# Early expert ids, feature-major row sums and modulation rows moved forward in a two-block transformer kernel

## Chip, cores and metric

The kernel runs on one core of a Trainium2 chip. The metric is the device time of one execution in microseconds, the median of several runs.

## The reference

A first block (attention with a causal mask, short convolution, PEER experts) is followed by a second block (feed-forward, retention with a context, Fourier branch, feed-forward). Everything is float32; 256 tokens and 256 context tokens of width 1024. All steps that are scaled, shifted or gated take their vectors from `silu(c) @ w_ada`: 12 pieces of 512 columns in the first block, 18 in the second. What the change touches:

```python
mod = jax.nn.silu(c) @ w_ada + b_ada
shift1, scale1, gate1, shift2, scale2, gate2 = jnp.split(mod, 6, axis=-1)
h = rms_norm(x, norm1_w) * (1.0 + scale1) + shift1
proj = h @ w_in                      # q, k, v, cb, cc, cx, iq, ik, iw
...
x = x + gate1 * (y_mix @ w_out)
h2 = rms_norm(x, norm2_w) * (1.0 + scale2) + shift2

# peer_ffn(h2), for each block of 128 tokens
q = (hb @ peer_wq).reshape(B, Q_BLOCK, PEER_HEADS, 2, PEER_HALF)
s = jnp.einsum('bqhpd,hpnd->bqhpn', q, peer_subkeys)
vals, idx = lax.top_k(s, PEER_TOPK)                  # 16 of 128 keys, twice
top_s, pos = lax.top_k(combo, PEER_TOPK)             # 16 of 256 pairs
expert = jnp.take_along_axis(ids, pos, axis=-1)      # 8 heads x 16 experts a token
g = jax.nn.softmax(top_s, axis=-1)
a = jax.nn.gelu(jnp.einsum('bqhkd,bqd->bqhk', peer_u[expert], hb))
y = jnp.einsum('bqhk,bqhkd->bqd', g * a, peer_v[expert])

x = x + gate2 * y
# second block begins: ctx and x each go through
x = x + 0.5 * g1x * swiglu(modulate(rmsnorm(x, norm_ffn1), sh1x, sc1x), w13_ffn1, w2_ffn1)
```

## The kernel before, in words

Activations lie feature-major, `x_t[feature within block, k, token]` with eight blocks `k` of 128 features. **Weights** stream through a ring of 2 MB slabs that SyncE (SP) loads in a fixed order, `slab_order`: SP waits until the slab that used the slot has been read and then issues one load. Slabs of `w_in`, `w_out` and `peer_wq` are split in four pieces each into a high part (ScalarE, `split_until`) and a low part (POOL before the gather, VectorE behind it), and each product is three matmuls. The order in which TensorE reads slabs is written out in its program; ScalarE's program repeats the same order for its copies out of PSUM.

**Modulation rows.** Each of the 30 pieces of `silu(c) @ w_ada` is a slab and a *row*: `mod_row_of(m)`, 8 matmuls of 32x512 (16 records, `psum<-ring,silu`). Rows are gathered in groups of two to four (`ROW_GROUPS`); when a group is complete and the next row has been done, `mod_turn` turns the group with 4 small matmuls (`psum<-early,small`) so that the vectors lie on partitions. `mod_steps(m0, m1)` does rows and the due turns. Rows 0 to 3 stand ahead of the input projection (`iq`, `q`, `k`, `v`, `cc`, `cx`, `cb`), rows 4 to 9 in it, 10 and 11 around the norm behind the output projection (`wo`), 12 to 17 between the four steps of the expert query (`pq`); row 18 (`SPARE`) has a slab of its own in `gap_slab[1]`, and 19 to 21 are ring slabs behind the query.

**Choice of the experts.** VectorE's `choose_experts(t)` handles one token tile of 128 in four groups of two heads (`top16`, the comparisons at L1769 and L1770), then computes all 128 ids a token (L1772) and publishes them (L1773, semaphore `ids`).

**Gather.** POOL copies eight ids a time (L1007) and issues one indirect DMA for each expert slot (L1017): 128 tokens, 8 KB each, 1 MB, 256 in all. Each row of `experts` holds `u` (first half) and `v` (second half). There are eight row buffers; a buffer comes free through `row_free_pe` (even rows) and `row_free_dve` (odd rows). The first tokens on both are given by VectorE ahead of the first dot, behind waits for the last key product and for row 18. Two rows make a batch, 128 batches. For a batch VectorE does two dots (L1838, `u` times `h2`), ScalarE the gelu (L1356), the gates (L1331) and a diagonal matrix of the even row's weights (L1335), TensorE adds the even row's `v` into two PSUM banks (2 matmuls of 128x512, token-major) and VectorE adds the odd row's into `y_of[t]` (L1845). At a tile's end VectorE adds the PSUM banks to `y_of[t]` (L1869), TensorE transposes the sum (`expert_turn`, L766) and VectorE adds it to `x_t` (`expert_residual`, L1792).

Between batches each engine takes steps of the **context's** feed-forward and of its `k` and `v` projections (108 chunks, `context()` on each engine), and VectorE the choice for the second tile. `ctx` itself is loaded by SP when the last `peer_wq` slab has been read.

**Tail.** Behind the gather come `squares_by_block("x1")` (8 matmuls with a matrix of ones, from ScalarE's squares, L1143), a root (L1035) and a reciprocal (L1488), row 22 out of `gap_slab[0]`, and the first feed-forward of the second block. Its first slab is loaded when the last even expert row has landed; then the gap slabs (each waits for both tokens of the buffers it overlays); then four loads of constants and two more slabs. Every matmul is issued through `mm` (L437).

```python
for half, bank in enumerate(sum_banks[t]):
    last = mm(psum[:, bank, :], diag[:, n % (GBUF // 2), :],
              rows[BATCH * n % GBUF][:, D + half * BANK:D + (half + 1) * BANK], b == 0, b == PER_TILE - 1)
last.then_inc(sem("row_free_pe"), 1)
```

## Time and profile before

| | us |
|---|---|
| median of 3 runs | 1847.63 (1844.91 to 1849.25) |
| the profiled execution, its own time | 1845.29 |
| its span, first to last instruction | 1843.5 |
| TensorE busy | 1619.5 (88%) |
| VectorE busy | 1219.8 (66%) |
| ScalarE busy | 701.6 (38%) |
| POOL busy | 452.2 (25%) |
| DMA, mean rate | 292 GB/s, 538.22 MB |

Engines in rows are PE (TensorE), PEld (its weight loads), DVE (VectorE), ACT (ScalarE), POOL (GpSimd), SP (SyncE). All times count from the span's start. Busy time in a row of matmuls counts records, which may be two for one instruction (`x16` are 8 matmuls). In brackets stands how long the engine was idle before an instruction, and what ended that. The gather runs from about 292 to 1050 us.

### The profile page before, as it was taken

What the parts mean: (1) busy time and instruction counts of PE and PEld (TensorE: products, weight loads), DVE (VectorE), ACT (ScalarE), POOL (GpSimd) and SP (SyncE); (2) the same over time, 40 slices, a digit from 0 to 9 for tenths busy, and PEclk for the clock granted to TensorE, in tenths of its full rate; (3) what the DMA queues carried; (4) which work ended last, traced back from release to release, by engine and by line L of the source; (5) the groups of instructions that cost most, each with busy time, mean ns of one, the idle gap of its engine ahead of it and who ended that gap; (6) DMA issues with size and microseconds to landing.
All of it is one profiled execution on the core that took longest, in us unless ns stands there. A gap on an engine that the chain in (4) does not pass through costs nothing.

```text
span 1843.5 us, 25165 instructions
## 1 busy us (share of the span) xinstructions
PE 1619.5 (88%) x9708; PEld 1296.9 (70%) x9708; DVE 1219.8 (66%) x1967; ACT 701.6 (38%) x1266; POOL 452.2 (25%) x342
## 2 busy tenths in 40 slices
PE   5999993888879878776998699999999999999997
PEld 3987771555646555544533289998999895989997
DVE  3795486887888877567577756565458447566554
ACT  4544342332233221123222356745443441444443
POOL 1664443443434534434445200000000000000000
PEclk8999996899989988888999799999999999999999
DMA  8556888999999999999999956645545550346542
GB/s 365 183 216 275 354 346 354 376 421 421 405 420 412 418 421 418 422 422 384 422 420 420 404 226 258 246 160 179 217 142 187 197 189 19 137 143 229 190 160 102
DMA packets 58001, 538.22 MB, mean 292 GB/s; under 512 B 6432, under 2 KB 6560, under 8 KB 7712
## 3 DMA queue, kind: packets, MB, share of 16 engines
q1 hardware_dynamic: 21024, 268.22, 37.4%
q0 software_dynamic: 36864, 268.45, 35.3%
q8 instruction: 76, 1.25, 0.3%
q14 instruction: 37, 0.30, 0.0%
HBM read 535.60 MB, written 1.05 MB: 291 GB/s over the span
## 4 chain that ended last, share of the span: by engine, by line
PE 51%; DMA 23%; DVE 14%; issue 7%; ACT 3%; POOL 1%; SPq 0%; POOLq 0%; DVEq 0%; ACTq 0%
PE psum L437 51%; DMA arena<-in_experts,idx_stage 20%; DVE arena L1845 2%; DMA ring<-in_w_ada 1%; POOL arena L1017 1%; DMA ring<-in_peer_wq 1%; DVE arena L1653 1%; DVE ring_r L1432 1%; DVE small L1770 1%; DMA ring<-in_w_in 0%; DVE arena L1769 0%; DMA ring<-in_w_ffn 0%; ACT h_t L1294 0%; ACT ring_r L1050 0%; DVE h_t L1512 0%
## 5 line engine op out<-in xcount | busy, mean ns | idle before, releaser
L1432 DVE TENSOR_TENSOR ring_r<-ring,ring_r 128x1024 fp32r<-128x1024 f32 (+1 forms) x240 | 287.0, 1207 | 270.9 <-ACT ring_r L1050 269.6
L437 PE MATMUL psum<-arena,small 128*128 128x512 f32 x544 | 303.5, 690 | 161.2 <-ACT small L1335 158.2
L1838 DVE CUSTOM_DVE_ANT_0 arena<-arena 128x1024 f32<-128x1024 f32 x256 | 313.8, 1226 | 179.7 <-DMA arena<-in_experts,idx_stage 174.3
L437 PE MATMUL psum<-small_r,ring_r 128*128 128x256 f32 x2304 | 415.6, 284 | 7.2 <-DVE h_t_r L1518 7.0
L1017 POOL DMA_INDIRECT arena<-in_experts,idx_stage x256 | 306.2, 1196 | 371.2 <-DVE arena L1845 172.1
L437 PEld LDWEIGHTS psum<-small_r,ring_r 128*128 128x128 f32 x2304 | 355.2, 189 | 14.8 <-issue 14.5
L1050 ACT ACTIVATE ring_r<-ring 128x1024 fp32r<-128x1024 f32 (+1 forms) x240 | 246.4, 1041 | 229.0 <-PE psum L437 178.4
L437 PE MATMUL psum<-arena_r,ring_r 128*128 128x256 f32 x2208 | 328.5, 283 | 3.2 <-DVE arena_r L1497 2.8
L437 PE MATMUL psum<-h_t_r,ring_r 128*128 128x256 f32 x1152 | 322.8, 280 | 0.0
L437 PEld LDWEIGHTS psum<-arena,small 128*128 128x128 f32 x544 | 111.5, 215 | 295.2 <-ACT small L1335 169.9
L437 PEld LDWEIGHTS psum<-arena_r,ring_r 128*128 128x128 f32 x2208 | 291.8, 190 | 3.8 <-DVE arena_r L1497 3.2
L1356 ACT ACTIVATE small<-small 128x2 f32<-128x2 f32 x128 | 26.0, 203 | 513.1 <-DVE small L1838 513.1
L437 PEld LDWEIGHTS psum<-h_t_r,ring_r 128*128 128x128 f32 x1152 | 218.7, 190 | 0.1
L437 PEld LDWEIGHTS psum<-h_t,ring 128*128 128x128 f32 x848 | 164.5, 194 | 52.2 <-issue 27.7
L437 PE MATMUL psum<-h_t,ring 128*128 128x256 f32 x848 | 195.4, 384 | 2.7 <-ACT h_t L1294 2.7
L1845 DVE SCALAR_TENSOR_TENSOR arena<-arena,small 128x1024 f32<-128x1024 f32 x128 | 164.5, 1285 | 4.6
L995 POOL TENSOR_TENSOR ring_r<-ring,upper 128x1024 fp32r<-128x1024 f32 x50 | 127.4, 2572 | 134.3 <-ACT upper L1050 94.7
L437 PE MATMUL psum<-arena_r,upper 128*128 128x256 f32 x768 | 144.0, 290 | 12.9 <-DVE arena_r L1518 8.4
L437 PEld LDWEIGHTS psum<-arena_r,upper 128*128 128x128 f32 x768 | 123.1, 196 | 16.6 <-issue 8.8
L437 PEld LDWEIGHTS psum<-arena,ring 128*128 128x128 f32 x352 | 70.2, 199 | 22.8 <-issue 13.9
L437 PE MATMUL psum<-arena,ring 128*128 128x256 f32 x352 | 83.6, 391 | 0.0
L1073 ACT ACTIVATE arena<-psum 128x512 f32<-128x512 f32 (+2 forms) x91 | 48.1, 545 | 76.6 <-PE psum L437 61.0
(234 smaller groups left out, 1416.4 us busy)
## 6 DMA issues: line engine op xcount, KB each, us to landing
ring<-in_w_ffn SPq DMA_DIRECT2D x33, 2048.0 KB
ring<-in_w_in SPq DMA_DIRECT2D x31, 2048.0 KB
ring<-in_w_ada SPq DMA_DIRECT2D x27, 2048.0 KB
ring<-in_w_ffn SPq DMA_DIRECT2D x24, 1408.0 KB
ring<-in_w_out SPq DMA_DIRECT2D x4, 2048.0 KB
ring<-in_peer_wq SPq DMA_DIRECT2D x4, 2048.0 KB
ring<-in_p_ret SPq DMA_DIRECT2D x4, 2048.0 KB
arena<-in_w_ada SPq DMA_DIRECT2D x3, 2048.0 KB, 12.7
```

Source lines behind the costliest of these rows:

```text
L437: return nc.tensor.matmul(o, a, b, start=first, stop=last)
L995: nc.gpsimd.tensor_tensor(whole(i, ring_r), whole(i, ring), upper(i).bitcast(F32), ALU.subtract).then_inc(lo_made, 1)
L1017: nc.gpsimd.indirect_dma_start(rows[slot % GBUF], None, dram["experts"], bass.IndirectOffsetOnAxis(ap=idx_stage[:, slot:slot + 1], axis=0) ...
L1050: nc.scalar.activation(upper(i), whole(i, ring), ACT.Copy).then_inc(hi_made, 1)
L1073: drain(nc.scalar.activation(dst, take(name)[:, 0:width], func, scale=scale))
L1356: nc.scalar.activation(acts[:, n % 8, :], dots[:, n % 8, :], ACT.Gelu_apprx_tanh).then_inc(sem("gelus"), 1)
L1432: nc.vector.tensor_tensor(whole(i, ring_r), whole(i, ring), upper(i).bitcast(F32), ALU.subtract).then_inc(lo_made, 1)
L1653: step(nc.vector.reciprocal(rs, rs))
L1770: step(nc.vector.tensor_reduce(hid_[:, a, some], hot, AX_X, ALU.add))
L1838: step(nc.vector.tensor_tensor_reduce(u, u, h2[:, n // PER_TILE, :], 1.0, 0.0, ALU.mult, ALU.add, dots[:, n % 8, s:s + 1]), sem("dots"))
L1845: STT(y_of[t], rows[(BATCH * n + 1) % GBUF][:, D:2 * D], weights[:, n % 8, 1:2], y_of[t], ALU.mult, ALU.add).then_inc(sem("row_free_dve"), 1)
```

## The change

It has six parts.

1. **Rows move forward.** `SPARE` becomes 21. Rows 4 and 5 stand behind `v`, 6 and 7 behind `cx`, 8 behind `cb`, 9 ahead of and 10 and 11 behind the attention's products, 12 ahead of `wo`, 13 and 14 around the norm, 15 to 20 between the steps of the query. Only 21, with the slab of its own, stays behind it.
2. **Early ids.** For the first tile the ids of the first six heads are published when the third of four groups is chosen, the last two heads' when the fourth is. POOL walks over a list of id ranges. The first tokens for row buffers are given by ScalarE behind its copy of row 21.
3. **ctx over POOL.** The load of `ctx` becomes an indirect DMA of POOL with the index `lane`, ahead of its gathers.
4. **Feature-major sums.** The even row's `v` is the stationary operand in 8 blocks of 128x128, the diagonal matrix the moving one, so that the sum stands feature-major in PSUM. The odd rows' sum `y_of[t]` is added into the same banks by 8 products with the identity. VectorE's two additions go. The last batch is done row by row: its odd row is also added by TensorE, behind `expert_turn(1, False)`.
5. **Half of the squares early.** Squares, sum, root and reciprocal of `x1` for tokens 0 to 127 are done between the context's steps in the gather; the tail keeps those of tokens 128 to 255.
6. `gap_slab[1]` is loaded behind the last sum, `yt1_1`.

```diff
-SPARE, GAP = 18, 22
+SPARE, GAP = 21, 22
...
-    first = (mods[:4] + w_in(0) + [("w_idx", 0, KD * 136)] + w_in(1) + w_in(2) + w_in(3) + mods[4:5] + w_in(4) + w_in(5)
-             + mods[5:6] + w_in(6) + mods[6:10] + out_proj + mods[10:12] + peer(0) + mods[12:14] + peer(1)
-             + mods[14:16] + peer(2) + mods[16:18] + peer(3) + mods[SPARE + 1:GAP])
+    first = (mods[:4] + w_in(0) + [("w_idx", 0, KD * 136)] + w_in(1) + w_in(2) + w_in(3) + mods[4:6] + w_in(4) + w_in(5)
+             + mods[6:8] + w_in(6) + mods[8:13] + out_proj + mods[13:15] + peer(0) + mods[15:17] + peer(1)
+             + mods[17:19] + peer(2) + mods[19:21] + peer(3))
...
+        published = [[PH // 2 - 1, PH // 2], [PH // 2]]
...
-            def squares_by_block(tag, sq=sq2, summed=1):
+            def squares_by_block(tag, sq=sq2, summed=1, tokens=slice(0, L)):
...
-                    last = mm(o[:, 0:L], ones[:], sq[:, k, :], k == 0, k == KD - 1)
+                    last = mm(o[:, tokens], ones[:], sq[:, k, tokens], k == 0, k == KD - 1)
...
+            def add_row(t, g, turn, first, last):
+
+                for j in range(KD):
+                    ins = mm(summed(t, j), rows[g % GBUF][:, D + j * P:D + (j + 1) * P], diag[:, turn % (GBUF // 2), :],
+                             first and j % 4 == 0, last and j % 4 == 3)
...
+            def expert_turn(t, last):
 
                 pe.wait_ge(sem("experts"), t + 1)
-                for i in range(2):
-                    o = begin(f"yt{t}_{i}", "dve")
-                    for j in range(4):
-                        last = nc.tensor.transpose(o[:, j * P:(j + 1) * P],
-                                                   y_of[t][:, (4 * i + j) * P:(4 * i + j + 1) * P], ident)
-                    ctx_end(f"yt{t}_{i}", last)
+                for j in range(KD):
+                    ins = mm(summed(t, j), y_of[t][:, j * P:(j + 1) * P], ident, False, last and j % 4 == 3)
...
+                pe.wait_ge(sem("sq_x1_first"), 1)
+                o = begin("ss_x1_first", "act")
+                for k in range(KD):
+                    last = mm(o[:, 0:P], ones[:], sq_first[:, k, :], k == 0, k == KD - 1)
...
-                for half, bank in enumerate(sum_banks[t]):
-                    last = mm(psum[:, bank, :], diag[:, n % (GBUF // 2), :],
-                              rows[BATCH * n % GBUF][:, D + half * BANK:D + (half + 1) * BANK], b == 0, b == PER_TILE - 1)
-                last.then_inc(sem("row_free_pe"), 1)
...
+                add_row(t, BATCH * n, n, b == 0, False).then_inc(sem("row_free_pe"), 1)
...
-            expert_turn(1)
-            squares_by_block("x1")
+            expert_turn(1, False)
+            pe.wait_ge(sem("diag"), BATCHES + 1)
+            add_row(1, BATCH * BATCHES - 1, BATCHES, False, True)
+            squares_by_block("x1", tokens=slice(P, L))
...
+            pool.wait_ge(sem("lane"), 1)
+            pool.wait_ge(*slab_free[slabs.index(("peer_wq", 3, SLAB))])
+            nc.gpsimd.indirect_dma_start(ctx_t.rearrange("p k t -> p (k t)"), None, dram["ctx"],
+                                         bass.IndirectOffsetOnAxis(ap=lane, axis=0)).then_inc(sem("ctx_landed"), 16)
...
+            lists = [(t, b0 * 2 * PSEL // ROUND, b1 * 2 * PSEL // ROUND) for t in range(NT)
+                     for b0, b1 in zip([0] + published[t], published[t])]
+            for known, (t, r0, r1) in enumerate(lists):
+                pool.wait_ge(sem("ids"), known + 1)
...
             mod_row_of(SPARE)
+            act.sem_inc(sem("row_free_pe"), GBUF // 2)
+            act.sem_inc(sem("row_free_dve"), GBUF // 2 + 1)
...
+                yield done_at["yt0_1"] + 2
+                act.wait_ge(*emptied("yt0_1"))
+                nc.scalar.activation(sq_first, x_t[:, :, 0:P], ACT.Square).then_inc(sem("sq_x1_first"), 1)
...
-                step(nc.vector.reciprocal(rstd[:], rstd[:]))
+                fresh = rstd[:, P:L] if tag == "x1" else rstd[:]
+                step(nc.vector.reciprocal(fresh, fresh))
...
+                    if g + 1 in published[t]:
+                        known = slice(([0] + published[t])[published[t].index(g + 1)] * 2 * PSEL, (g + 1) * 2 * PSEL)
+                        step(STT(id_f[:, known], hid_[:, 0, known], float(PK), hid_[:, 1, known], ALU.mult, ALU.add))
+                        step(nc.vector.tensor_copy(ids[:, t * SLOTS + known.start:t * SLOTS + known.stop], id_f[:, known]),
+                             sem("ids"))
                     yield
-                step(STT(id_f, hid_[:, 0, :], float(PK), hid_[:, 1, :], ALU.mult, ALU.add))
-                step(nc.vector.tensor_copy(ids[:, t * SLOTS:(t + 1) * SLOTS], id_f), sem("ids"))
...
-                    for half, bank in enumerate(sum_banks[t]):
-                        y = y_of[t][:, half * BANK:(half + 1) * BANK]
-                        step(TT(y, y, psum[:, bank, :], ALU.add), sem("experts") if half else chain)
```

How it moves instructions, first on TensorE between the last input slab (`cb`) and the first product of the output projection. Before (`ring,silu` is a modulation row, `early,small` a turn, `early,h_t` the turned probabilities, `arena,ones` a sum of squares, `arena` 128x128 the attention's products):

```order
L437 MATMUL psum<-ring,silu 32x512 x8
L701 MATMUL psum<-early,h_t 128x128 x16
L437 MATMUL psum<-ring,silu 32x512 x8
L437 MATMUL psum<-arena 128x128 x12
L437 MATMUL psum<-arena,ones 128x256 x4
L437 MATMUL psum<-arena 128x128 x12
L437 MATMUL psum<-ring,silu 32x512 x8
L437 MATMUL psum<-early,small 128x4 x4
L437 MATMUL psum<-arena,ones 128x256 x4
L437 MATMUL psum<-ring,silu 32x512 x8
L437 MATMUL psum<-arena_r,upper_53 128x256 x2
```

With the change, for the same stretch:

```order
L442 MATMUL psum<-ring,silu 32x512 x8
L442 MATMUL psum<-early,small 128x4 x4
L707 MATMUL psum<-early,h_t 128x128 x16
L442 MATMUL psum<-ring,silu 32x512 x8
L442 MATMUL psum<-arena 128x128 x12
L442 MATMUL psum<-arena,ones 128x256 x4
L442 MATMUL psum<-arena 128x128 x12
L442 MATMUL psum<-ring,silu 32x512 x8
L442 MATMUL psum<-early,small 128x2 x4
L442 MATMUL psum<-ring,silu 32x512 x8
L442 MATMUL psum<-arena,ones 128x256 x4
L442 MATMUL psum<-ring,silu 32x512 x8
L442 MATMUL psum<-early,small 128x2 x4
L442 MATMUL psum<-arena_r,upper_53 128x256 x2
```

Between the attention's products and the sum of squares stand two rows (10 and 11) where one stood (8). One turn has become three: that of rows 4 to 7 has gone ahead of the probabilities, and those of 8 and 9 and of 10 and 11 are new here, the last of them directly ahead of the output projection.

SP's queue around the last `w_in` slab, before (each row a load, in brackets what it waits for):

```order
L964 DMA ring<-in_w_in 128x4096 [waits group_done] x2
L964 DMA ring<-in_w_ada 128x4096 [waits group_done]
L964 DMA ring<-in_w_in 128x4096 [waits group_done] x2
L964 DMA ring<-in_w_ada 128x4096 [waits group_done]
L964 DMA ring<-in_w_in 128x4096 [waits piece_done]
L964 DMA ring<-in_w_ada 128x4096 [waits group_done] x2
L964 DMA ring<-in_w_ada 128x4096 [waits piece_done]
L964 DMA ring<-in_w_ada 128x4096 [waits group_done]
L964 DMA ring<-in_w_out 128x4096 [waits piece_done]
L964 DMA ring<-in_w_out 128x4096 [waits group_done]
```

With the change:

```order
L980 DMA ring<-in_w_in 128x4096 [waits group_done] x2
L980 DMA ring<-in_w_ada 128x4096 [waits group_done] x2
L980 DMA ring<-in_w_in 128x4096 [waits group_done] x2
L980 DMA ring<-in_w_ada 128x4096 [waits piece_done] x2
L980 DMA ring<-in_w_in 128x4096 [waits group_done]
L980 DMA ring<-in_w_ada 128x4096 [waits group_done]
L980 DMA ring<-in_w_ada 128x4096 [waits piece_done]
L980 DMA ring<-in_w_ada 128x4096 [waits group_done] x2
L980 DMA ring<-in_w_ada 128x4096 [waits piece_done]
L980 DMA ring<-in_w_out 128x4096 [waits group_done]
L980 DMA ring<-in_w_out 128x4096 [waits piece_done]
```

Two modulation slabs instead of one stand ahead of the last `w_in` slab, and five (rows 8 to 12) instead of four (rows 6 to 9) between it and `w_out`.

The end of the gather on TensorE, before: the last context products (`ring,h_t`), the rest of the row sums, the transposes (L766), the sum of squares of `x1` and row 22.

```order
L437 MATMUL psum<-ring,h_t 128x512 x4
L437 MATMUL psum<-arena,small 128x512 x20
L766 MATMUL psum<-early,arena 128x128 x8
L437 MATMUL psum<-small,ones 128x256 x8
L437 MATMUL psum<-arena,silu 32x512 x8
```

With the change (80 are ten even rows of eight products, `early,arena` adds the odd rows' sum, the next eight add the last odd row):

```order
L442 MATMUL psum<-ring,h_t 128x512 x4
L442 MATMUL psum<-small,arena 128x128 x80
L442 MATMUL psum<-early,arena 128x128 x8
L442 MATMUL psum<-small,arena 128x128 x8
L442 MATMUL psum<-small,ones 128x128 x8
L442 MATMUL psum<-arena,silu 32x512 x8
```

Each row of experts is eight products of 128x128 where it was two of 128x512, the transposes have become additions in the same banks, and the sum of squares has half of the columns.

## Rows read from the trace of the kernel before

**Rows 1.** Stretches: length, busy us (instructions) by engine, PEclk, DMA share, GB/s.
```profile
57.00:107.00 50.00, 48.93 (x347) 42.44 (x346) 46.92 (x77) 28.34 (x47) 35.27 (x14) 1.00 0.51 188
...
290.00:300.00 10.00, 0.00 (x0) 0.00 (x0) 1.44 (x5) 1.59 (x2) 3.91 (x5) 0.50 0.46 170
...
330.00:340.00 10.00, 8.73 (x19) 4.55 (x20) 9.79 (x24) 6.21 (x17) 3.88 (x4) 0.72 0.59 220
340.00:850.00 510.00, 417.89 (x1410) 277.82 (x1409) 391.53 (x673) 132.18 (x374) 217.93 (x193) 0.91 1.01 418
```

**Rows 2.** Timeline of PE: start us, us, operation, [idle before <-releaser].
```profile
107.23 0.37 PE L437 MATMUL psum<-arena 64*128 64x128 f32 x1 [1.30 <-DVE arena L1654]
...
155.12 1.92 PE L437 MATMUL psum<-ring,silu 128*32 128x512 f32 x16
156.98 1.05 PE L437 MATMUL psum<-early,small 128*128 128x4 f32 x8
157.89 1.97 PE L437 MATMUL psum<-arena,ones 128*128 128x256 f32 x8
...
164.02 0.47 PE L437 MATMUL psum<-arena_r,upper 128*128 128x256 f32 x2 [2.31 <-POOL ring_r L995]
```

**Rows 3.** Timeline of DVE, end of the choice and first dots.
```profile
275.58 0.49 DVE L1721 MAX8 small<-arena 128x8 f32<-128x128 f32 x2
...
291.29 0.29 DVE L1777 TENSOR_TENSOR small<-small 128x128 f32<-128x128 f32 x1
301.00 1.23 DVE L1838 CUSTOM_DVE_ANT_0 arena<-arena 128x1024 f32<-128x1024 f32 x1 [9.42 <-DMA arena<-in_experts,idx_stage]
...
304.80 1.23 DVE L1838 CUSTOM_DVE_ANT_0 arena<-arena 128x1024 f32<-128x1024 f32 x1 [2.56 <-DMA arena<-in_experts,idx_stage]
...
319.78 1.23 DVE L1838 CUSTOM_DVE_ANT_0 arena<-arena 128x1024 f32<-128x1024 f32 x1 [1.17 <-DMA arena<-in_experts,idx_stage]
```

**Rows 4.** Timeline of POOL, first gathers.
```profile
292.00 0.19 POOL L1007 COPY idx_stage<-ids 128x8 uint32 x1 [29.83 <-DVEq L1829]
295.36 1.12 POOL L1017 DMA_INDIRECT arena<-in_experts,idx_stage  x1 [3.17 <-issue]
...
334.87 1.90 POOL L1017 DMA_INDIRECT arena<-in_experts,idx_stage  x1 [10.79 <-PE psum L437]
```

**Rows 5.** L1769, 230 to 292, then 292 to 680: ns min/median/max, start.
```profile
L1769 DVE TENSOR_TENSOR arena<-arena,small x8: 691/693/2769, 231.0 to 289.0; 128x512 f32<-128x512 f32 x8
L1769 DVE TENSOR_TENSOR small<-small x8: 691/692/693, 385.4 to 612.5; 128x512 f32<-128x512 f32 x8
```

**Rows 6.** Timeline of PE, and its group of row sums, 342 to 1040.
```profile
217.83 2.05 PE L437 MATMUL psum<-arena 128*128 128x128 f32 x16
219.63 0.48 PE L437 MATMUL psum<-arena_r,upper 128*128 128x256 f32 x2
...
989.33 1.88 PE L437 MATMUL psum<-arena,small 128*128 128x512 f32 x4
991.04 3.60 PE L437 MATMUL psum<-ring,h_t 128*128 128x512 f32 x8
...
994.48 1.88 PE L437 MATMUL psum<-arena,small 128*128 128x512 f32 x4
...
L437 PE MATMUL psum<-arena,small 128*128 128x512 f32 x483 | 269.4, 687 | 119.2 <-ACT small L1335 116.2 <-issue 3.0
```

**Rows 7.** Chain of waits (first line), then timelines of ACT, PE and DVE, the tail.
```profile
1042.00 8.19 DMA ring<-in_w_ffn
...
1054.09 2.54 ACT L1143 ACTIVATE small<-x_t 128x256 f32<-128x256 f32 x8
...
1054.63 5.92 PE L437 MATMUL psum<-small,ones 128*128 128x256 f32 x16 [2.92 <-ACT small L1143]
...
1061.17 1.75 DVE L1488 RECIPROCAL rstd<-rstd 128x256 f32<-128x256 f32 x1 [4.12 <-ACT rstd L1035]
```

**Rows 8.** The page, costliest groups: weight loads.
```profile
L437 PEld LDWEIGHTS psum<-small_r,ring_r 128*128 128x128 f32 x2304 | 355.2, 189 | 14.8 <-issue 14.5
```

143 lines of the change are left out of this document (85 added, 58 removed).

## The prediction

> **What bounds the kernel now.** I read the table of stretches first, then the timelines of TensorE, VectorE and GpSimd (POOL) at its edges. The span falls into three parts. In the **head**, up to about 290 us, TensorE is the bound: 48.93 of 50 us busy, with DMA at a share of 0.51 [rows 1]. In the **gather**, rows of the experts stream in; from 340 to 850 us DMA stands at 1.01 of its engines and 418 GB/s, while TensorE (417.89 of 510) and VectorE (391.53) have room [rows 1]. Between the two lies a hole: from 290 to 300 us DMA is at 0.46 and VectorE works 1.44 us of 10 [rows 1]. The gather therefore ends when its 256 MB are through, and starts when VectorE has published the expert ids. In the **tail**, behind 1042 us, a chain of short steps leads to the first feed-forward: slab, pieces, squares, root, reciprocal.
>
> **Head: three more rows ahead of the ids.** Rows 4 to 12 instead of 4 to 9 now stand before the output projection. One row of TensorE takes 156.98 − 155.12 = 1.86 us from start to start [rows 2], so three cost 5.6. The order shows two more turns before that projection and one fewer behind it. A turn is 1.05 us long and 157.89 − 156.98 = 0.91 from start to start; I take 1.0 where one is added and 0.9 where one is saved. One added turn lies right before the squares of attention and counts, +1.0. The other lies behind them, ahead of the output projection, where TensorE waits 2.31 us for POOL's pieces [rows 2]: nothing. The one that goes from behind the projection gives −0.9. Row 5 now stands before the second projection `cc`, and TensorE waits 1.30 us there for VectorE's mask [rows 2]; the row's 1.86 us fill that wait: −1.3. Sum +5.6 + 1.0 − 1.3 − 0.9 = +4.4, taken as **+4.5**. Bounds: +3, if the 2.31 us wait takes in more of it (row 12 moves ahead of that wait too), and +8, if a slab is late or the last `w_in` slab, now asked for behind two more rows, is split late (5.6 + 2.0 + some of a row). The three slabs' 6.3 MB take 15.0 us at the 418 GB/s of [rows 1]; 49% of 50 us idle at that stage hides them. The same rows vanish from behind the query, where nobody but DMA was short.
>
> **Ids and the first dots.** VectorE's last step of tile 0's choice starts at 291.29 and takes 0.29; the first dot starts at 301.00, after 9.42 us of waiting for a row; then come waits of 2.56 and 1.17 us [rows 3]. Now ids of three of four groups are published when the third group ends, 275.58 [rows 3], plus 0.5 us for the two added operations (under the 0.29 us each of the 128x128 operation at 291.29) plus 4.5 of head: about 280.6. POOL copied at 292.00 and issued at 295.36 with 3.17 us in between [rows 4]; the same from 280.6 on puts the first issue at 284, and with the 5.6 us from issue to dot seen before (301.00 − 295.36) the row is there at 289.6. VectorE is then the bound: it ends its choice at 291.6 + 4.5 + 0.5 = 296.6 and starts its dots then, 4.4 us before 301.00. The waits inside the first batches, 2.56 + 1.17 = 3.7, go as well, since rows have landed in all eight buffers. So the gather's state at its VectorE-bound stretch comes **8.1 us** earlier. That stretch is real: from 330 to 340 VectorE is busy 9.79 of 10 with DMA at 0.59, and POOL stands 10.79 us before 334.87 for a buffer that TensorE holds [rows 1, 4]. Behind it DMA is the bound, so the lead carries to the last row. Bounds: nothing, if a later token holds POOL, to −15.0 below.
>
> What speaks against this: while the fourth group is chosen, POOL now issues gathers. `L1769`, two of which stand in each group, took 0.69 us in the median but 2.77 once, in the stretch in which POOL still subtracts; with gathers running, from 292 to 680 us, all eight took 0.691 to 0.693 [rows 5]. So I add nothing. The Trainium skill, "SBUF — State Buffer", section "Who interferes with whom", says that a VectorE operation with two SBUF inputs contends with a GpSimd operation that reads SBUF, over a port that one holds at a time. If issuing a gather were such a read, the fourth group's two `L1769` would each grow by 2.1 us, and with 4.2 us less gain the kernel would come to 1840.2. The trace of the gather speaks against it.
>
> **Row sums with the features on the partitions.** For an even row TensorE now issues 8 products of 128x128, 16 records, in place of 2 of 128x512. 16 records of 128x128 took 219.63 − 217.83 = 1.80 us [rows 6]; the present four take 991.04 − 989.33 = 1.71 [rows 6]. So +0.1 us a batch, 128 batches, 12 us of work. TensorE idles 119.2 us before exactly these products from 342 to 1040 us [rows 6], so it costs nothing; without that cover it would cost 12. The period with a context chunk is now 994.48 − 989.33 = 5.15 us and would be 5.24; DMA's pace is (1042 − 301) / 128 = 5.8 us a batch, on average.
>
> **Tail.** The landing of the feed-forward slab holds: it is asked for at 1042.00 and is there 8.19 us later [rows 7], when the last even row is in; that doesn't move against the last row. ACT splits it and squares from 1054.09 on, 2.54 us; TensorE's sum of squares takes 5.92 from 1054.63; VectorE's reciprocal 1.75 [rows 7]. Half of the tokens are now done in the gather. TensorE: −5.92 / 2 = −3.0, of which I take 2.6, since it starts only with the first squares. VectorE: −0.9. ACT's squares run ahead of TensorE's sum and give nothing themselves. Sum **−3.5**, bounds −2 and −5. The row-by-row last batch and the dropped additions end earlier than before and are covered by the slab's landing. The second gap slab, asked for later, and ctx over POOL's queue move only loads with slack: nothing.
>
> **Sum.** +4.5 − 8.1 − 3.5 is −7.1 against the old times; but the 4.4 us at the first dot already hold the head's +4.5 (without it they would be 8.9). So the head is not counted twice: −8.1 − 3.5 = −11.6. From the profiled execution's 1845.3 that gives 1833.7; the median of the runs, 1847.6, lies 2.3 higher, so I forecast **1836.0**.
>
> **Rivals.**
> (a) The head costs 8 instead of 4.5 and half of the two waits stays: 3.5 + 1.9 = 5.4 us above the forecast, 1841.4. For it: POOL's queue of subtractions and the ring slots are tied to the row order. Against: a DMA share of 0.51. Chance 0.15.
> (b) DMA is the bound from the first row on. Then the three slabs of 15.0 us that leave the stretch behind the query count in full instead of 8.1: 1829.1. Against: the share of 0.59 at 330 to 340 [rows 1]. Chance 0.10.
> (c) The lead is lost. A token that comes late, or a batch in the VectorE-bound stretch that waits for something else, puts the gather back where it was; the tail remains at best, and a head that is longer eats it: 1844 to 1849. Chance 0.10. That the change doesn't do what it says belongs here: the early list would bring nothing if POOL sat behind its load of ctx.
> (d) **Slower.** The short products don't hide their weight loads. One load of 128x128 takes 189 ns [rows 8]. If 16 of them stood bare, a row's sum would cost 3.0 us, and TensorE's period with a chunk 3.44 + 3.0 = 6.5 us against DMA's 5.8. With 108 chunks and 20 batches without, 108 × 6.5 + 20 × 5.0 = 802 us against 741: +61 less 12, near 1896. It decides from 5.8 − 3.44 = 2.4 us a row on. Against it: the transposes of [rows 6], 112 ns a record with loads of the same size. The Trainium skill, "TensorE: Matmul & The Clock Gate", section "Back-to-back issue gap", gives some 81 ns for a sustained pair of load and product at 128 columns, where a lone product needs 56. Scaling the present 1.71 us by that ratio is 2.5 us, an estimate by that page, and would put the kernel just over the point. The row of 1.80 us is a direct measurement, so I give this 0.06.
>
> **How the numbers follow.** Forecast 0.59, (a) 0.15, (b) 0.10, (c) 0.10, (d) 0.06. The forecast's own bounds, from the head (+3.5, −1.5), the tail (±1.5) and the median (±2), are about 1831 to 1841. The range 1827 to 1846 adds (a), (b) and the better part of (c). 0.2% is 3.7 us, about what a measurement of this kernel can tell from no change: faster is below 1843.9, which holds the forecast, (a), (b) and a little of (c), less what of them could miss by more: 0.79. Same 0.12, from (c) and the upper end of (a). Slower 0.09, from (d) and a head that isn't paid back.
>
> **What would show it.** The first `L1838` at about 296.6, its second and fourth without a wait; POOL's first gather near 284; the last step of the choice 5 us later than before; a record of the 128x128 sums at 112 ns and TensorE's period below 5.3 us; still idle time of some 100 us before them; DMA at 1.0 from about 332; the last even row near 1034; TensorE's sum of squares for `x1` 3 us or less, the reciprocal 0.9. The prediction is wrong if TensorE is busy without gaps between 340 and 1030, if the choice ends later than 298, or if POOL's first gathers wait for a token.

## The result and the profile after

The change measured 1836.5 us (median of 5 runs, 1831.41 to 1842.43), against 1847.63 before. The ratio is 0.9935 with a 95% interval from 0.9919 to 0.9952. A repeat of the changed kernel gave 1835.29 against 1849.76, ratio 0.9923 (0.9910 to 0.9936). The forecast was 1836.0.

The profiled execution of the change took 1837.43 us (span 1835.6), only 7.9 less than that of before. Why the two profiles differ by less than the medians is taken up below: the profiled head of before was short, that of the change long.

The table of stretches of the changed kernel, with the columns of [rows 1]:

```profile
57.00:107.00 50.00, 50.00 (x359) 42.52 (x360) 45.72 (x77) 26.14 (x44) 32.76 (x13) 1.00 0.49 188
290.00:300.00 10.00, 0.00 (x0) 0.00 (x0) 9.59 (x33) 0.23 (x2) 5.73 (x6) 0.50 0.99 409
330.00:340.00 10.00, 7.98 (x55) 7.32 (x54) 9.76 (x27) 5.99 (x16) 4.36 (x5) 1.00 0.73 265
340.00:850.00 510.00, 420.25 (x2431) 380.31 (x2429) 389.52 (x671) 136.84 (x378) 215.49 (x191) 0.92 1.01 417
```

The hole at 290 to 300 us has gone: DMA at 0.99 instead of 0.46, VectorE at 9.59 us of 10 instead of 1.44. From 340 on the gather is DMA's as before. The head is the other side, still TensorE's. Its timelines around the output projection, first ScalarE, then TensorE (compare [rows 2]), then SP's issue of the `w_out` slabs:

```profile
165.45 2.00 ACT L1075 ACTIVATE upper<-ring 128x1024 fp32r<-128x1024 f32 x2 [4.09 <-DMA ring<-in_w_out]
...
164.09 1.99 PE L442 MATMUL psum<-arena,ones 128*128 128x256 f32 x8
166.01 1.92 PE L442 MATMUL psum<-ring,silu 128*32 128x512 f32 x16
168.20 1.05 PE L442 MATMUL psum<-early,small 128*128 128x2 f32 x8 [0.26 <-ACT small L1098]
172.49 0.47 PE L442 MATMUL psum<-arena_r,upper 128*128 128x256 f32 x2 [3.23 <-DVE arena_r L1548]
...
152.25 9.46 SPq L980 DMA_DIRECT2D ring<-in_w_out  x2
```

From the start of the attention's sum of squares to the first product of the output projection passed 6.13 us before (157.89 to 164.02) and pass 8.40 now (164.09 to 172.49). ScalarE stood 4.09 us for the slab of `w_out`. TensorE's wait ahead of the projection has grown from 2.31 to 3.23 us, although a turn was put into it.

VectorE, end of the third group's ids and the first dots (compare [rows 3]), and POOL (compare [rows 4]):

```profile
285.37 0.26 DVE L1825 SCALAR_TENSOR_TENSOR small<-small 128x96 f32<-128x96 f32 x1
285.67 0.21 DVE L1826 CAST ids<-small 128x96 uint32<-128x96 f32 x1
301.88 1.23 DVE L1891 CUSTOM_DVE_ANT_0 arena<-arena 128x1024 f32<-128x1024 f32 x1
303.15 1.23 DVE L1891 CUSTOM_DVE_ANT_0 arena<-arena 128x1024 f32<-128x1024 f32 x1
...
316.36 1.22 DVE L1891 CUSTOM_DVE_ANT_0 arena<-arena 128x1024 f32<-128x1024 f32 x1
323.87 1.22 DVE L1891 CUSTOM_DVE_ANT_0 arena<-arena 128x1024 f32<-128x1024 f32 x1
...
286.30 0.18 POOL L1032 COPY idx_stage<-ids 128x8 uint32 x1 [6.88 <-DVE ids L1826]
287.57 0.97 POOL L1042 DMA_INDIRECT arena<-in_experts,idx_stage  x1 [1.08 <-issue]
331.15 0.94 POOL L1042 DMA_INDIRECT arena<-in_experts,idx_stage  x1 [10.18 <-PE psum L442]
```

POOL copies ids 0.4 us after they are known and issues 1.3 us later, 14.3 us ahead of the first dot. No dot waits for a row up to 323.87; before, five of the first eight waited, 13.8 us in all (9.42, 2.56 and 1.17 of [rows 3], 0.43 and 0.26). POOL still stands 10.18 us for TensorE before 331.15. The choice ends directly ahead of the first dot, at 301.9: later than the 298 us behind which the prediction had called itself wrong. The section on why the forecast held takes this up.

The row sums on TensorE, one period with a context chunk and the group from 332 to 1031 us (compare [rows 6]):

```profile
900.21 1.95 PE L442 MATMUL psum<-small,arena 128*128 128x128 f32 x16
902.00 3.62 PE L442 MATMUL psum<-h_t,ring 128*128 128x256 f32 x16
...
907.24 3.60 PE L442 MATMUL psum<-ring,h_t 128*128 128x512 f32 x8
...
L442 PE MATMUL psum<-small,arena 128*128 128x128 f32 x1922 | 269.2, 300 | 112.1 <-ACT small L1366 111.9
```

Sixteen records take 1.79 us, the period is 907.24 − 902.00 = 5.24 us, and TensorE idles 112.1 us before these products.

The tail: SP, ScalarE, TensorE, VectorE (compare [rows 7]):

```profile
1039.13 0.33 SPq L980 DMA_DIRECT2D ring<-in_w_ffn  x1
1051.19 1.69 ACT L1168 ACTIVATE small<-x_t 128x128 f32<-128x128 f32 x8
1051.63 2.02 PE L442 MATMUL psum<-small,ones 128*128 128x128 f32 x16 [3.36 <-ACT small L1168]
1057.47 0.36 PE L442 MATMUL psum<-small_r,ring_r 128*128 128x256 f32 x1 [1.97 <-DVE h_t_r L1569]
1054.66 0.95 DVE L1539 RECIPROCAL rstd<-rstd 128x128 f32<-128x128 f32 x1 [1.53 <-ACT rstd L1060]
```

From the issue of the first feed-forward slab to its first product 22.77 us passed before (1042.00 to 1064.77), 18.34 now.

### The profile page after: what moved, and what is told of

It is laid out like the page before. It is cut to its first block, busy times and chain, and to the rows that moved or that the text cites. A ratio compares the mean times of both kernels' runs of the same rounds, so it can differ in the third digit from the quotient of the medians.

```text
span 1835.6 us, 28337 instructions
## 1 busy us (share of the span) xinstructions
PE 1621.9 (88%) x11292; PEld 1456.0 (79%) x11292; DVE 1212.0 (66%) x1968; ACT 704.7 (38%) x1272; POOL 447.5 (24%) x343
## 4 chain that ended last, share of the span: by engine, by line
PE 55%; DMA 22%; DVE 11%; issue 6%; ACT 4%; POOL 1%; SPq 0%; POOLq 0%; DVEq 0%; ACTq 0%
PE psum L442 54%; DMA arena<-in_experts,idx_stage 18%; DMA ring<-in_w_ffn 2%; DVE arena L1898 2%; DMA ring<-in_w_ada 1%; POOL arena L1042 1%; DMA ring<-in_peer_wq 1%; DVE ring_r L1482 1%; DMA ring<-in_w_out 1%; DVE arena_r L1548 1%; ACT ring_r L1075 1%; DVE small L1822 0%; DVE arena L1821 0%; ACT h_t L1321 0%; DVE h_t L1563 0%
## 5 line engine op out<-in xcount | busy, mean ns | idle before, releaser
L442 PE MATMUL psum<-small,arena 128*128 128x128 f32 x2064 | 292.4, 302 | 147.2 <-ACT small L1366 147.0
L442 PEld LDWEIGHTS psum<-small,arena 128*128 128x128 f32 x2064 | 280.3, 215 | 173.1 <-ACT small L1366 143.4
L1042 POOL DMA_INDIRECT arena<-in_experts,idx_stage x256 | 301.6, 1178 | 376.3 <-DVE arena L1898 166.7
L442 PEld LDWEIGHTS psum<-h_t,ring 128*128 128x128 f32 x848 | 160.3, 194 | 24.0 <-ACT h_t L1321 3.8
L1075 ACT ACTIVATE upper<-ring 128x1024 fp32r<-128x1024 f32 x52 | 53.6, 1053 | 62.8 <-DMA ring<-in_peer_wq 28.8
## 6 DMA issues: line engine op xcount, KB each, us to landing
ring<-in_w_ada SPq DMA_DIRECT2D x27, 2048.0 KB, 11.1
arena<-in_w_ada SPq DMA_DIRECT2D x3, 2048.0 KB, 12.6
```

Source lines behind the costliest of these rows:

```text
L442: return nc.tensor.matmul(o, a, b, start=first, stop=last)
L1042: nc.gpsimd.indirect_dma_start(rows[slot % GBUF], None, dram["experts"], bass.IndirectOffsetOnAxis(ap=idx_stage[:, slot:slot + 1], axis=0) ...
L1075: nc.scalar.activation(upper(i), whole(i, ring), ACT.Copy).then_inc(hi_made, 1)
```

## Experiments

Each was run on the chip beside the kernel before. For the comparisons below I use six places read from the timeline of every profile (us): modulation row 4, the last row ahead of the output projection, the first row behind it, VectorE's last cast of ids of tile 0, the first dot, and the dot of the last even row. Profiles of one kernel differ by up to 5 us in these places, so stretches between two places are compared, not the places themselves.

| profile | row 4 | last ahead | first behind | last ids | first dot | last even dot |
|---|---|---|---|---|---|---|
| before | 98.1 | 159.8 | 190.3 | 290.82 | 301.00 | 1042.16 |
| before, again | 99.6 | 161.3 | 191.8 | 295.95 | 306.30 | 1048.61 |
| rows only | 98.1 | 164.7 | 197.1 | 299.54 | 309.83 | 1051.82 |
| change | 99.4 | 166.0 | 200.6 | 301.13 | 301.88 | 1039.29 |
| change, again | 101.2 | 167.8 | 201.2 | 301.67 | 302.41 | 1039.99 |
| full squares | 99.6 | 166.2 | 197.9 | 297.12 | 297.87 | 1035.66 |
| ctx by SP | 98.0 | 164.6 | 197.1 | 297.71 | 298.46 | 1035.70 |
| late ids | 100.4 | 167.0 | 200.9 | 299.43 | 307.19 | 1050.57 |
| rows back | 99.5 | 161.2 | 194.3 | 294.91 | 295.65 | 1042.99 |
| choice later | 99.4 | 166.0 | 199.9 | 299.10 | 299.85 | 1036.67 |
| row 12 later | 99.8 | 162.7 | 195.4 | 303.65 | 304.39 | 1040.82 |
| pieces behind the root | 99.9 | 162.7 | 198.0 | 302.49 | 303.23 | 1040.92 |
| the same, choice later | 98.2 | 161.0 | 193.8 | 299.85 | 300.59 | 1035.97 |
| sums doubled | 99.7 | 166.3 | 201.3 | 301.42 | 302.16 | 1111.19 |

### The two kernels again

> The changed kernel itself once more, for a second profile and a better median. The profiled execution of the change is 7.9 us under that of before (1837.43 against 1845.29), the medians are 11.1 apart. Theory A (the profile is typical): the gain is 8 to 9 us. Theory B (the medians are typical): 11 to 12 us. In the profile, rows at the same places as in the first one within 0.5 us, except that the start of the head may differ by 1.3 us, since the fourth modulation row ran at a lower granted clock in one of the two profiles (3.29 us against 1.93).

Measured: 1835.29 (5 runs, 1834.17 to 1839.44), ratio 0.9923; its profiled execution took 1839.44. The medians are 14.5 us apart here, more than theory B had, and theory A is out. Single executions of the change ranged from 1831.4 to 1842.4, so one profiled execution says little about the gain. Row 4 stood 1.8 us later than in the first profile, where 1.3 had been allowed.

> The kernel before itself, for a second profile. Within one kernel the heads of the profiles so far differ by up to 4.5 us (first dot of the changed kernel at 301.9, 302.4 and 297.9), in two stretches: the first four rows (granted clock 0.81 to 0.92 up to 36 us) and the output projection (31.7 to 34.6 us from the last row before it to the first behind it). Theory A (the profile of before had a short head): this one has its row 4 at 99 to 101 us instead of 98.1 and that stretch longer than 30.5 us, and its first dot at 303 to 306 instead of 301.0. Theory B (the stretch is longer because of the moved rows): 30.5 us again within 0.5.

Measured: 1849.15 (12 runs), ratio 1.0005 (0.9994 to 1.0016), profiled 1848.3. Row 4 at 99.6 as theory A had it, and the first dot at 306.30, 5.3 us later than in the first profile. But the projection's stretch was 30.5 us again, as theory B had it; the other 3.6 us came behind it, between the first row behind the projection and the ids (104.1 us against 100.5). So the first profile's head was shorter than this one, and not in the place that I had named. What made the 3.6 us isn't shown. The first 36 us differ in the granted clock as well; rows back and then the change again, with a mean clock of 0.93 and 0.81 there, the columns as in [rows 1]:

```profile
0.00:36.00 36.00, 16.31 (x88) 7.68 (x88) 9.37 (x31) 11.02 (x16) 0.20 (x4) 0.93 0.96 399
0.00:36.00 36.00, 18.08 (x88) 8.14 (x88) 8.05 (x30) 10.31 (x15) 0.20 (x4) 0.81 0.95 400
```

Row 4 stands at 99.5 in the one and 101.2 in the other, with the same work ahead of it. The mean clock doesn't order the profiles, though: row 4 stood at 98.1 with 0.89 (before) and at 99.4 with 0.86 (change), so it is at most a part of the difference.

### The rows alone, and all but the rows

```diff
-SPARE, GAP = 18, 22
+SPARE, GAP = 21, 22
```
(the first experiment is the kernel before with this, the slab order and all `mod_steps` of the change; the second is the inverse edit on the changed kernel)

> The kernel before with only the modulation rows moved. Theory A (rows ahead of the query cost the head 4.9 us, and what they take off the DMA behind the query is worth nothing while the ids come late and nothing waits for DMA there): +3 to +6 us over before, 1852 to 1855. Theory B (the three slabs that leave the stretch behind the query are worth more than the head costs): 1840 to 1847.

Measured: 1856.38 (7 runs, 1852.63 to 1858.64), ratio 1.0040 (1.0026 to 1.0055), 7 us slower, 1 more than theory A had at most. From row 4 to the last row ahead of the projection it takes 66.6 us where before takes 61.7, +4.9, the same in every profile with all of the rows moved. The first dot still waits:

```profile
309.83 1.22 DVE L1838 CUSTOM_DVE_ANT_0 arena<-arena 128x1024 f32<-128x1024 f32 x1 [9.53 <-DMA arena<-in_experts,idx_stage]
```

and from the last ids to the last even dot pass 752.3 us, against 751.3 and 752.7 before. So the moved rows give nothing back while the ids are late. The slowdown is put down to the head, since nothing else in the table grew.

> Only the modulation rows go back to their old places (4 to 9 before the output projection, 18 with its own slab, 19 to 21 behind the query); all else stays as changed. Theory A (the head pays: the choice ended 9.6 us later with the rows moved, and that is what bounds the first dot): the choice ends at about 292 instead of 301.9, the gather ends some 5 to 8 us earlier than in the changed kernel, about 1829 to 1832 us. Theory B (the three slabs behind the query are worth their 15 us of DMA): first rows land late, the dots wait for them, and the time is that of the changed kernel or up to 7 us more.

Measured: 1837.94 (5 runs, 1837.04 to 1843.32), ratio 0.9938 (0.9925 to 0.9950), 1 to 3 us over the change by the medians, with intervals that overlap. The last ids came at 294.9, 3 us later than theory A had the end of the choice and 6 to 7 earlier than in the change; the gain did not come, as theory B had it. VectorE's second dot, and the stretches of DMA:

```profile
301.75 1.22 DVE L1891 CUSTOM_DVE_ANT_0 arena<-arena 128x1024 f32<-128x1024 f32 x1 [4.86 <-DMA arena<-in_experts,idx_stage]
...
290.00:300.00 10.00, 0.00 (x0) 0.00 (x0) 6.48 (x14) 1.94 (x4) 0.95 (x1) 0.50 1.01 432
300.00:330.00 30.00, 12.50 (x66) 11.46 (x67) 23.12 (x49) 9.58 (x23) 7.51 (x7) 0.67 1.01 418
330.00:340.00 10.00, 8.88 (x47) 8.33 (x47) 9.79 (x24) 5.54 (x14) 4.43 (x5) 0.78 0.48 170
```

The first dot starts 0.7 us behind the last ids, the second waits 4.86 us for its row, with DMA at 1.01: the gathers share it with the feed-forward slabs behind the three late rows (SP issues them from 271.3 to 284.3 us, in the change from 259.4 to 277.8). From the last ids to the last even dot pass 748.1 us, against 738.2 and 738.3 in the changed kernel and 751.3 before. Of the 13 to 14 us that early ids and moved rows win together there, early ids alone (with the other parts of the change) win 3 to 5, moved rows alone none. In the whole time the rows also cost the head some 5 us, so that moving them is worth 1 to 3 us net, which these runs don't tell from nothing.

### Early ids

```diff
-        published = [[PH // 2 - 1, PH // 2], [PH // 2]]
+        published = [[PH // 2], [PH // 2]]
```

> Only the early list of ids goes: the first tile's ids are published once, when the fourth group is chosen. Theory A (the early list brings the whole gain at the start): the first gather is issued at about 303, the first dot waits until 308 to 310 instead of starting at 301.9, the waits of 2.6 and 1.2 us inside the first batches come back, and the time rises by 9 to 12 us, to about 1847. Theory B (the gather is bound by its row buffers at 315 to 331 us anyway): less than 4 us more.

Measured: 1847.39 (12 runs, 1844.1 to 1853.8), ratio 0.9987 (0.9976 to 0.9998): 12 us over the change's repeat, 11 over its first median. VectorE's first dots:

```profile
307.19 1.23 DVE L1891 CUSTOM_DVE_ANT_0 arena<-arena 128x1024 f32<-128x1024 f32 x1 [7.00 <-DMA arena<-in_experts,idx_stage]
310.50 1.23 DVE L1891 CUSTOM_DVE_ANT_0 arena<-arena 128x1024 f32<-128x1024 f32 x1 [2.07 <-DMA arena<-in_experts,idx_stage]
```

Theory A, at its upper end. The first gather was issued at 301.4, the first dot starts at 307.2, and from the last ids to the last even dot pass 751.1 us. Rows only, which also lacks parts 3 to 6, took 752.3 there: these parts are worth about 1 us in that stretch, no more than profiles of one kernel differ there.

### Squares of all tokens in the tail

```diff
-            squares_by_block("x1", tokens=slice(P, L))
+            squares_by_block("x1")
-            norm_hi("x1", 2, mod2_v[:, 0, :, 0], ["yt1_0", "yt1_1"], tokens=slice(P, L))
+            norm_hi("x1", 2, mod2_v[:, 0, :, 0], ["yt1_0", "yt1_1"])
...
-                fresh = rstd[:, P:L] if tag == "x1" else rstd[:]
+                fresh = rstd[:]
```

> The tail squares, sums and roots all 256 tokens again; the early half is computed and not used. Theory A (half of the work is half of the time, as forecast): +3.5 us, TensorE's sum of squares near 5.9 us again. Theory B (TensorE's 5.92 us before were the lower clock; behind the new row-by-row products it is at full clock, and its sum only follows ScalarE's squares): TensorE's sum under 3 us with all columns, ScalarE +0.9, VectorE +0.8, in all +1.7 us.

Measured: 1838.83 (6 runs, 1831.12 to 1842.7), ratio 0.9938 (0.9917 to 0.9959); the interval reaches from 1 us under the change's repeat to 7 over it, so the place is read from the trace. TensorE's sum of squares, then the first product:

```profile
1047.97 5.25 PE L442 MATMUL psum<-small,ones 128*128 128x256 f32 x16 [4.40 <-ACT small L1168]
1057.44 0.36 PE L442 MATMUL psum<-small_r,ring_r 128*128 128x256 f32 x1 [2.37 <-DVE h_t_r L1569]
```

The slab was issued at 1035.51, so 21.93 us passed to that product, against 18.34 and 19.04 in the change: +3.2. Theory A, by the size. On the clock both theories were too simple. With all columns the sum took 5.25 us, with a mean granted clock of 0.70 over it; with half of them it took 2.02 at 1.00 in the first profile of the change, but in the second it lost the clock too (0.63):

```profile
1052.51 3.05 PE L442 MATMUL psum<-small,ones 128*128 128x128 f32 x16 [3.70 <-ACT small L1168]
```

### The price of the row sums

```diff
-                add_row(t, BATCH * n, n, b == 0, False).then_inc(sem("row_free_pe"), 1)
+                add_row(t, BATCH * n, n, b == 0, False)
+                add_row(t, BATCH * n, n, False, False).then_inc(sem("row_free_pe"), 1)
```

> The changed kernel with the eight products of every even row issued twice into the same banks (the even rows are then added twice). It prices the cover over the row sums. Theory A (16 records take 1.8 us at full clock and nothing shows of them beside DMA): the added 128 x 1.8 = 230 us are 118 more than TensorE's 112 us of idle time before these products, so the time rises by 110 to 140 us, TensorE without gaps, DMA's share in the gather down to 0.86. Theory B (weight loads stand bare once products follow each other): a pair of sums takes over 4.8 us, and the time rises by 200 us or more.

Measured: 1909.93 (2 runs), ratio 1.0332 (1.0306 to 1.0358). Timeline of TensorE, the group of row sums from 340 to 1090 us, and the stretch of [rows 1]:

```profile
900.87 3.73 PE L442 MATMUL psum<-small,arena 128*128 128x128 f32 x32
904.44 3.62 PE L442 MATMUL psum<-h_t,ring 128*128 128x256 f32 x16
...
L442 PE MATMUL psum<-small,arena 128*128 128x128 f32 x3742 | 438.6, 277 | 12.6 <-ACT small L1367 12.6
...
340.00:850.00 510.00, 510.00 (x3597) 482.92 (x3596) 363.64 (x636) 123.82 (x350) 185.22 (x176) 1.00 0.97 389
```

32 records take 3.57 us, 112 ns each, so theory B falls. The idle time is down to 12.6 us and TensorE is busy for all of 510 us. But the time rose by 74 us over the change, not by 110 to 140, and DMA's share fell to 0.97, not 0.86. TensorE's mean granted clock from 340 to 850 us went from 0.92 to 1.00. From 340 us to the last context products and sums TensorE was busy for 577.5 of 691 us in the change and for 744.7 of 761 here: 167 us more, for added products of 128 × 1.79 = 229. The other 62 us were saved by records that had run at the lower clock (a record of the sums took 140 ns on average in the change, 117 here), and gaps took up 97. The cover over the row sums is larger than the idle time in the trace.

### ctx over SP

```diff
-            nc.gpsimd.indirect_dma_start(ctx_t.rearrange("p k t -> p (k t)"), None, dram["ctx"],
-                                         bass.IndirectOffsetOnAxis(ap=lane, axis=0)).then_inc(sem("ctx_landed"), 16)
...
+                if replaced is not None and slabs[replaced][:2] == ("peer_wq", 3):
+                    sp.dma_start(ctx_t.rearrange("p k t -> p (k t)"), dram["ctx"]).then_inc(sem("ctx_landed"), 16)
```

> The changed kernel with ctx loaded by SP again, behind the third feed-forward slab. Forecast: nothing (within 1.5 us). The rival: POOL's first gather was held by its load of ctx, which waits for the last peer_wq slab (POOL idles 6.4 us before it at 278.3), so without it POOL is ready earlier; but the first gather waits for the ids at 285.7 in any case.

Measured: 1834.93 (4 runs), ratio 0.9923 (0.9901 to 0.9945), the same as the change's repeat. The forecast holds: ctx over POOL neither costs nor gains.

### Attempts at a faster one

```diff
-    return (n + 1) * 2 // 5
+    return max(0, (n - 7) // 2)
```

> The changed kernel, with VectorE's choice for the second token tile begun at batch 9 instead of batch 2 and done a little faster, so that 5 us of it leave the stretch from 315 to 340 us. Theory A (VectorE bounds the gather's first 45 us, DMA idles 6 us in them): the DMA-bound state comes 4 to 5 us earlier and the time falls by as much, to 1831. Theory B (TensorE's late release of the row buffers bounds there: POOL waited 10.2 us for it before 331.2): less than 1.5 us gained.

Measured: 1834.5 (6 runs, 1831.65 to 1834.7), ratio 0.9919 (0.9904 to 0.9934), within the interval of the change. The ninth dot came 19.5 us behind the first instead of 22.0, yet from the last ids to the last even dot pass 737.6 us instead of 738.3. By this profile theory B: of a lead of 2.5 us, 0.7 is left. The last run of this section has the same edit and kept more.

```diff
-             + mods[6:8] + w_in(6) + mods[8:13] + out_proj + mods[13:15] + peer(0) + mods[15:17] + peer(1)
+             + mods[6:8] + w_in(6) + mods[8:12] + out_proj + mods[12:15] + peer(0) + mods[15:17] + peer(1)
...
-            mod_steps(12, 13, False)
...
-            mod_steps(13, 14)
+            mod_steps(12, 14)
```

> The changed kernel with row 12 and the turn ahead of the output projection moved behind it. Theory A (the first w_out slab lands late, at 164 instead of 154.5 us, since five modulation slabs are loaded ahead of it at 5 us each while TensorE uses a row up in 1.9): it lands 5 us earlier, the output projection begins 2 to 4 us earlier against row 11, and after the row's own 1.9 us the ids come 0.5 to 2 us earlier. Theory B (a row costs its 1.86 us wherever it stands): no change of the ids, within 0.5 us.

Measured: 1840.47 (6 runs), ratio 0.9952 (0.9933 to 0.9971), by the medians 4 to 5 us slower than the change, with intervals that still overlap. TensorE at the projection and at the norm, ScalarE at the norm:

```profile
168.72 0.47 PE L442 MATMUL psum<-arena_r,upper 128*128 128x256 f32 x2 [2.21 <-DVE arena_r L1546]
205.89 1.65 PE L442 MATMUL psum<-arena,ones 128*128 128x256 f32 x3 [5.14 <-ACT arena L1167]
...
203.53 2.00 ACT L1074 ACTIVATE upper<-ring 128x1024 fp32r<-128x1024 f32 x2 [11.95 <-DMA ring<-in_peer_wq]
```

The projection begins 6.1 us behind row 11 instead of 10.3, and ScalarE no longer waits for `w_out`: theory A's first half, though 2.9 of the 4.2 us are only the row and the turn that have gone from there. But the first `peer_wq` slab now lands one slab later, ScalarE waits 11.95 us for it with two squares of the norm behind it in its queue, and TensorE waits 5.14 for these. From row 4 to the last ids pass 203.8 us, against 201.7 and 200.5 in the change: the ids come later, not earlier.

The next run's edit, against this one:

```diff
-                    between={KD - 2: lambda: split_until(first_peer + 1), KD: lambda: mod_steps(12, 14)})
+                    between={KD: lambda: mod_steps(12, 14), "root": lambda: split_until(first_peer + 1)})
```

> Row 12 behind the output projection as in the run before, and ScalarE's first two pieces of peer_wq are split behind the norm's root instead of ahead of its last two squares. Theory A (in the run before, ScalarE stood 11.95 us for that slab with two squares behind it, and TensorE 5.1 us for them; the slab's place in the queue is the cost): TensorE's wait of 5.1 us goes, the query's first product comes at 207 to 209 for a row 11 at 162.5, the ids come 1 to 3 us earlier than in the changed kernel, about 1833. Theory B (the pieces are then late for the query instead): the query waits for POOL, and nothing is gained.

Measured: 1840.92 (6 runs), ratio 0.9956 (0.9939 to 0.9973). The wait at the norm has gone, and this one has come ahead of the query:

```profile
213.03 0.77 PE L442 MATMUL psum<-arena_r,upper 128*128 128x256 f32 x2 [6.95 <-DVE arena_r L1569]
```

Nothing is gained, as theory B had it, but not for its reason: TensorE waits for VectorE, and ScalarE did not wait for the slab when it began its pieces (206.16). The time went into VectorE's first three steps of `h_t`, here beside POOL's subtractions of these pieces, and below in the change, without them:

```profile
207.04 5.45 DVE L1563 SCALAR_TENSOR_TENSOR h_t<-x_t,cols,rstd 128x256 f32<-128x256 f32 x3
207.30 4.91 POOL L1013 TENSOR_TENSOR ring_r<-ring,upper 128x1024 fp32r<-128x1024 f32 x2 [15.39 <-ACT upper L1074]
...
206.87 1.28 DVE L1563 SCALAR_TENSOR_TENSOR h_t<-x_t,cols,rstd 128x256 f32<-128x256 f32 x3
```

They took 5.45 us instead of 1.28, 4.2 us that stand directly ahead of the query. The wait for the slab itself had gone.

> The run before plus the later choice for the second tile, the version meant to beat both kernels. By the two effects (1 to 3 us, and 0.8 us from the last ids to the last even row as measured): 1831 to 1834.

Measured: 1839.55 (6 runs, 1834.08 to 1841.72), ratio 0.9952 (0.9935 to 0.9969): the forecast of 1831 to 1834 failed, since the first of its two effects had not come. The ninth dot again came 19.5 us behind the first, and from the last ids to the last even dot pass 736.1 us, against 738.4 in the run that it is built on: here 2.3 of the 2.5 us were kept. No version beat the change by more than its interval.

## Why the forecast held, point by point

**The total** is right, to 0.5 us against the first median, and the sum was of the right terms; that it is so close is in part luck. For a profiled execution of the change the prediction had 1833.7, and the profile took 1837.43. It had also called itself wrong if the choice ended later than 298 us. The choice ended at 301.9 and 302.4, and with it the first dot came 5 us later than forecast (301.9 for 296.6) and the last even row as well (1039.3 for 1034). So by its own sign the head is where it was wrong. A part of the 5 us is the profiles: the first profile of before had its last ids at 290.8, the second at 296.0, and both of the change lie some 2 us above the average of the heads with moved rows. With all profiles the terms are these.

**Head, forecast +4.5 (bounds 3 to 8).** Between row 4 and the last row ahead of the projection the moved rows cost 4.9 us, in each profile. My terms up to there were 5.6 + 1.0 + 0 − 1.3 = 5.3. The last ids of seven heads with these rows in the table (rows only, the change twice, full squares, ctx by SP, late ids, choice later) stand at 299.4 on average; before, twice, at 293.4. With 0.4 us of it for the added operations of early ids that is +5.6 for the head, 1 us over the forecast (with the head of the doubled sums as an eighth, +5.9). As single heads of one kernel lie up to 5 us apart, the 1 us is not clear of noise; the wait that it contains is. **The step that failed** is that 49% of idle DMA hides the slabs. From the start of the last row ahead of the projection to the projection's first product 4.2 us pass in both profiles of before, and 5.1 to 6.9 in the eight with moved rows. Five modulation slabs in a row, 5 us of DMA each (2.1 MB at 418 GB/s), stand ahead of `w_out`; TensorE uses a row up in 1.86 us. SP asked for `w_out` at 152.25 instead of 144.22, and the slab was there 13 us later; ScalarE waited 4.09 us for it, and the turn that I put down as free, inside the 2.31 us wait, was not. The idle DMA lay elsewhere: in the change its share was 0.69 and 0.47 from 110 to 120 and to 130 us, while SP waited for slots of the ring, and 0.92 to 1.01 from 150 to 165, when `w_out` was on its way. The first experiment with row 12 shows that it is the slab's place in the queue: with one slab fewer ahead of `w_out` the projection starts earlier, and the wait has moved to `peer_wq`, the next slab that is needed. The second removes that wait and meets another, of VectorE beside POOL.

**Start of the gather, forecast −8.1.** From the last ids to the last even dot: 751.3 and 752.7 before, 738.2 and 738.3 (full squares 738.5, ctx by SP 738.0) after, −13.8. Less the head and the added operations (+6.0) that is −7.8. The mechanism is as forecast: no dot waits for a row, the choice itself is the bound, and without the early list all of it goes (+12 us). What the forecast did not have is that it needs both parts: with the rows back in place the ids come 5 us sooner, but the gathers then share DMA with slabs that come behind three late rows. In the forecast I had left that DMA without a price in the sum; rival (b) had put 15 us on it. The experiment puts 9.8 us on it (748.1 against 738.3), less 5 for the head; by the medians 1 to 3 us of that remain.

**Row sums, forecast nothing.** 1.79 us a row and a period of 5.24 were forecast to 0.01, and the 112.1 us of idle time are there. Rival (d) fell on both: 112 ns a record also when they follow without a gap. No run takes the row sums alone back; that they cost nothing rests on the idle time, on their price with doubled sums and on late ids against rows only. The ratio of a sustained pair to a lone product that the Trainium skill gives at 128 columns ("TensorE: Matmul & The Clock Gate", "Back-to-back issue gap"), from which I had the 2.5 us, does not show here: the measured 1.79 decides.

**Tail, forecast −3.5 (2 to 5).** From the slab's issue to the first product 22.8 and 23.9 us before, 18.3 and 19.0 after, −4.7. Halved squares are 3.2 of it by experiment. Some 1.0 of the other 1.5 lies in the same sum of squares: with all columns it took 5.92 and 6.58 us before, at a granted clock of 0.62 in the first, against 5.25 at 0.70 in that experiment. From the slab's issue to ScalarE's first piece nothing moved (8.3 and 8.5 us before, 8.3 after). ctx over POOL costs nothing, as forecast.

**Sum.** −7.8 − 4.7 = −12.5, against −11.6 forecast and −11.1 and −14.5 measured by the two pairs of medians. The sum leaves out everything behind the first feed-forward product, 778.7 and 774.1 us before, 778.1 and 778.7 in the change. That stretch differs by 4.6 us between two profiles of one kernel, so the sum is no better than a few us, and its closeness to the medians proves no single term.

**What an early lead is worth.** The forecast said that a lead at the VectorE-bound stretch carries to the last row. For the change it did. All that the change won there it had by the ninth dot: 36.5 and 36.3 us behind the last ids before, 22.7 in both profiles of the change; from there to the last even dot pass 714.9 and 716.4 before, 715.4 and 715.6 now. The later choice made 2.5 us there and kept 0.7 in one run and 2.3 in the other. Profiles of the change without that edit lie between 737.2 (row 12 later) and 738.5 us from the last ids to the last even dot, so two profiles can't settle whether this lead carries. Why the first kept less I haven't shown.

## What to carry to other kernels

A weight slab in a ring costs its transfer time in the place where it stands, not on the average of the stretch: ahead of a slab that is needed soon, count slabs times their 5 us against the engine's use of them, and don't read idle DMA as cover. In one stretch two edits can be worth nothing and 3 to 5 us alone, and 13 together, when one removes the wait and the other clears the transfers that would take its place; test the pair and each alone, and set against it what each costs elsewhere (here 5 us of head). And when two single profiles are compared, compare each stretch from its own start, and take a second profile of the kernel before: its head alone differed by 5 us.

## What was not expected of the hardware

TensorE's granted clock rose with its load. In the gather it was 0.92 with 112 us of idle time, 1.00 with the sums doubled; the added 230 us of work cost 74. The sum of squares in the tail ran at 126 ns a record (2.02 us for 16) with half of the columns in the first profile of the change, 3.36 us of idle time ahead of it, and at 191 (3.05 us) in the second, with 3.70 ahead; with all columns and 4.40 ahead it ran at 328 (5.25 us). The granted clock over these sums was 1.00, 0.63 and 0.70.

VectorE's operation with two inputs in SBUF ahead of the projection took 1.32 us before and 3.15 in the change:

```profile
160.24 1.32 DVE L1497 TENSOR_TENSOR arena_r<-arena,arena_r 128x1024 fp32r<-128x1024 f32 x1 [2.92 <-ACT arena_r L1262]
158.11 5.66 POOL L995 TENSOR_TENSOR ring_r<-ring,upper 128x1024 fp32r<-128x1024 f32 x2 [22.57 <-ACT upper L1050]
...
169.19 3.15 DVE L1548 TENSOR_TENSOR arena_r<-arena,arena_r 128x1024 fp32r<-128x1024 f32 x1 [7.60 <-ACT arena_r L1287]
166.59 7.99 POOL L1014 TENSOR_TENSOR ring_r<-ring,upper 128x1024 fp32r<-128x1024 f32 x3 [26.83 <-ACT upper L1075]
```

POOL subtracts beside it in both; what differs is which came first. Before, VectorE began at 160.24 and POOL's second subtraction at 160.44; that one took 3.33 us, where the one ahead of it had taken 2.37. In the change POOL's second subtraction ran from 168.91 to 171.26 when VectorE began at 169.19, and VectorE ended 1.1 us behind it. So the one that began second was the longer one. Here the Trainium skill's rule ("SBUF — State Buffer", "Who interferes with whom"), that such an operation contends with a GpSimd operation that reads SBUF, agrees with the trace. In the choice's fourth group, where POOL issues gathers, all stayed at 0.69 us.
